# A hybrid encoder on one core: single-row norm, one addition ahead of a head, and wide products in two of the sample's projections

## The reference, cut to what matters

```
for layer in range(2):
    h = rms_norm(x, norm_mix)
    y = even mixer (S5 and GLA heads) @ ev_w_out    # layer 0
    y = diff_attention(h, od_w_in, ...) @ od_w_out  # layer 1
    x = x + y
    h = rms_norm(x, norm_cross); x = x + cross_attention(h, rms_norm(mem), x_w_q, x_w_kv, x_w_o)
    h = rms_norm(x, norm_mlp);   x = x + square(relu(h @ mlp_w1)) @ mlp_w2

def diff_attention(h, w_in, ...):
    q, k, v = split(h @ w_in, 3)                    # 1024 columns each
    q = rms_norm(q per head and half, 64 wide) * 64 ** -0.5
    k = rms_norm(k per head and half, 64 wide)
    ...
def cross_attention(h, m, ...):
    q = rms_norm(h @ w_q per head, 256 wide) * 256 ** -0.5
```

## Time and profile before

| | |
|---|---|
| median of 3 runs | 2398.26 us (2398.01 to 2398.31) |
| the profiled execution | 2397.84 us |
| its span, first to last instruction | 2396.1 us |
| TensorE matmuls busy | 2384.5 us (100%), 13751 of them |
| TensorE weight loads busy | 2019.0 us (84%) |
| VectorE busy | 1548.1 us (65%), 2626 instructions |
| ScalarE busy | 1169.3 us (49%), 2070 instructions |
| granted TensorE clock | 1.00 of full speed |

### The profile page before, as it was taken

The page is one execution under the profiler, slowest core; times in us unless marked ns, Lnnn a source line. Parts: engine busy times, 40 slices in busy tenths (PEclk is TensorE's granted clock), DMA queues, the critical chain, the costliest instruction groups (busy, mean ns, idle before and its releaser), DMA issues.

```text
span 2396.1 us, 34669 instructions
## 1 busy us (share of the span) xinstructions
PE 2384.5 (100%) x13751; PEld 2019.0 (84%) x13751; DVE 1548.1 (65%) x2626; ACT 1169.3 (49%) x2070; POOL 0.2 (0%) x4
## 2 busy tenths in 40 slices
PE   9999999999999999999999999999999999999999
PEld 6988877888889888998788888888888898888887
DVE  8999668776577876664665448858985565533332
ACT  5334455555435565545453436636764453533432
POOL 0000000000000000000000000000000000000000
PEclk9999999999999999999999999999999999999999
DMA  5445533563224553443234223233234323423322
GB/s 201 106 98 163 211 110 96 171 205 117 69 88 150 193 189 127 134 140 98 79 96 168 88 94 122 93 97 97 91 104 146 118 80 120 126 97 97 97 97 88
DMA packets 109696, 291.30 MB, mean 122 GB/s; under 512 B 18944, under 2 KB 40576, under 8 KB 108256
## 3 DMA queue, kind: packets, MB, share of 16 engines
q1 hardware_dynamic: 100832, 264.83, 34.6%
q10 hardware_dynamic: 8704, 24.25, 3.2%
HBM read 267.45 MB, written 19.50 MB: 120 GB/s over the span
## 4 chain that ended last, share of the span: by engine, by line
PE 86%; DVE 3%; ACT 1%; issue 0%; DVEq 0%; ACTq 0%
PE ps L1524 65%; PE ps L1510 5%; PE ps L1515 3%; PE ps L1638 2%; PE ps L1595 2%; PE ps L1620 2%; PE ps L1662 1%; PE ps L1651 1%; DVE wlo L1486 1%; PE ps L1608 0%; DVE ringP L1929 0%; PE ps L1669 0%; PE ps L2034 0%; PE ps L2101 0%; PE ps L1538 0%
## 5 line engine op out<-in xcount | busy, mean ns | idle before, releaser
L1481 ACT ACTIVATE whi<-wraw 128x1024 fp32r<-128x1024 f32 x430 | 451.9, 1052 | 173.8 <-PE ps L1524 127.2
L1524 PE MATMUL ps<-in_hP,whi 128*128 128x512 f32 x1336 | 533.2, 399 | 1.7 <-DVE in_lP L1936 0.9
L1486 DVE TENSOR_TENSOR wlo<-wraw,whi 128x1024 fp32r<-128x1024 f32 x430 | 522.3, 1217 | 0.2
L1524 PE MATMUL ps<-in_hP,wlo 128*128 128x512 f32 x1336 | 520.9, 390 | 0.0
L1524 PE MATMUL ps<-in_lP,whi 128*128 128x512 f32 x1336 | 520.2, 389 | 0.0
L1524 PE MATMUL ps<-hid_P,whi 128*128 128x512 f32 x1024 | 316.9, 391 | 0.0
L1524 PEld LDWEIGHTS ps<-in_hP,whi 128*128 128x128 f32 x1336 | 250.8, 188 | 60.5 <-issue 5.9
L1524 PEld LDWEIGHTS ps<-in_hP,wlo 128*128 128x128 f32 x1336 | 250.7, 188 | 53.4
L1524 PEld LDWEIGHTS ps<-in_lP,whi 128*128 128x128 f32 x1336 | 251.0, 188 | 51.8 <-issue 1.4
L1524 PE MATMUL ps<-in_S,whi 128*128 128x256 f32 x1536 | 285.4, 287 | 0.5 <-DVE x L1869 0.5
L1869 DVE TENSOR_TENSOR x<-ps,x 128x256 f32<-128x256 f32 (+1 forms) x192 | 106.7, 556 | 261.2 <-PE ps L1524 259.5
(11 more groups left out here) (506 smaller groups left out, 3509.1 us busy)
## 6 DMA issues: line engine op xcount, KB each, us to landing
wraw<-wt SPq DMA_DIRECT2D x432, 512.0 KB, 3.5
wraw<-wt ACTq DMA_DIRECT2D x17, 512.0 KB, 4.1
k_scratch<-region_P SPq DMA_DIRECT2D x16, 256.0 KB, 3.1
v_scratch<-vtmp SPq DMA_DIRECT2D x32, 128.0 KB, 3.6
x<-x_in SPq DMA_DIRECT2D x4, 768.0 KB, 6.7
x<-x_in SPq DMA_DIRECT2D x2, 1536.0 KB, 7.1
mix_mem<-mem_in ACTq DMA_DIRECT2D x1, 2048.0 KB, 15.2
region_S<-k_scratch ACTq DMA_DIRECT2D x2, 1024.0 KB, 7.5
```

The source lines that it names most:

```text
L1481: nc.scalar.activation(whi[:, (n + 3) % NHI, :, :], wraw[:, ws(n), :, :], ACT.Copy).then_inc(wh.sem, 1)
L1486: nc.vector.tensor_tensor(wlo[:, ws(n), :, :], wraw[:, ws(n), :, :], whi[:, (n + 3) % NHI, :, :].bitcast(F32), ALU.subtract).then_inc(wr.s ...
L1524: last = nc.tensor.matmul(ps[:, m % 2, 0:N[prod.g]], w_[:, k, :], x_[:, k, :], start=(k == 0 and j == 0), stop=(k == KT - 1 and j == 2))
```

## The change

It has four parts. (1) `WIDE` gains `q1` and `din`, and `Product` lets kinds "q" and "qkv" of the sample be wide. So the sample's queries of the second layer (8 tiles) and the 24 tiles of the differential input projection take the wide form. The halves are added by a VectorE reduce (`dve_halves`), which writes queries and keys to where ScalarE's copy went, and values to `ring`; it also frees the bank. ScalarE then squares from SBUF, and does not copy any more. The residue of the square moves from the tile's own place on VectorE to the slot behind it (`dve_square_low`). (2) The prompt's norm ahead of its `q1` is cut in `ONES` and no longer in `FINE`. (3) `added` holds also beside a "fin" of the prompt, which is the case for the first sample tile of `eo` alone. (4) In a slot where the step of a query pair goes first, a wide tile is taken first too; no wide tile stands in such a slot.

```diff
-            WIDE = {WT[n] for n in ("dn00", "dn01", "dn02", "dn03", "dout", "o0", "up01", "up02", "up03", )}
+            WIDE = {WT[n] for n in ("dn00", "dn01", "dn02", "dn03", "dout", "o0", "up01", "up02", "up03", "q1", "din", )}
...
-                    if g == "S" and kind in ("res", "up") and w0 in WIDE:
+                    if g == "S" and kind in ("res", "up", "q", "qkv") and w0 in WIDE:
...
             run(Product("res", "P", WT["dout"], dP.ready, norm=nP))
-            later([], *norm_steps(nP, FINE))
+            later([], *norm_steps(nP, ONES))
             mS.run(10)
...
+                elif prod.kind == "q" and prod.wide is not None:
+                    a.wait_ge(tf[b].sem, m // 2 + 1)
+                    if i >= 2:
+                        a.wait_ge(z["tqd"].sem, prod.tq + i // 2)
+                    nc.scalar.activation(ring[g][:, i % 2, :], qx[g][:, i, :], ACT.Square).then_inc(z["sqd"].sem, 1)
...
+                elif prod.kind == "qkv" and prod.wide is not None:
+                    if i < 16:
+                        a.wait_ge(tf[b].sem, m // 2 + 1)
+                        if i >= 2:
+                            a.wait_ge(z["ssum"].sem, prod.stats[i - 2].sum)
+                        act_chain(nc.scalar.activation(ring[g][:, i % 2, :], (dq, dk)[i // 8][g][:, i % 8, :], ACT.Square))
+                        if i >= 1:
+                            a.wait_ge(z["ssum"].sem, prod.stats[i - 1].sum)
+                        nc.scalar.activation(sq_h[g][:, :], ring[g][:, i % 2, :], ACT.Copy).then_inc(z["sqd"].sem, 1)
...
+            def dve_halves(v, t, to):
+                prod, i, m = t
+                b = m % 2
+                v.wait_ge(td.sem, m + 1)
+                nc.vector.tensor_reduce(to, ps[:, b, :].rearrange("p (z t) -> p t z", z=2), AX.X, ALU.add).then_inc(tf[b].sem, 1)
+
+            def dve_square_low(v, t):
+                prod, i, m = t
+                v.wait_ge(gs["S"]["sqd"].sem, prod.sq + i + 1)
+                nc.vector.tensor_tensor(sq_l["S"][:, i % 2, :], ring["S"][:, i % 2, :], sq_h["S"][:, :].bitcast(F32), ALU.subtract)\
+                    .then_inc(gs["S"]["sql"].sem, 1)
...
+                elif prod.kind == "q" and prod.wide is not None:
+                    dve_halves(v, t, qx[g][:, i, :])
+                elif prod.kind == "qkv" and prod.wide is not None and i < 16:
+                    dve_halves(v, t, (dq, dk)[i // 8][g][:, i % 8, :])
+                elif prod.kind == "qkv" and prod.wide is not None:
+                    if i < 18:
+                        v.wait_ge(z["ssum"].sem, prod.stats[i - 2].sum)
+                    else:
+                        v.wait_ge(z["vtr"].sem, prod.vtr + i - 17)
+                    dve_halves(v, t, ring[g][:, i % 2, :])
...
-                            step[0] == "nfin" and step[1].g == "P" for step in steps)
+                            step[0] == "nfin" and step[1].g == "P" or step[0] == "fin" and step[1].g == "P" for step in steps)
...
+                        if before is not None and before[0].kind == "qkv" and before[0].wide is not None and before[1] < 16:
+                            dve_square_low(v, before)
                         if added:
                             dve_tile(v, t)
                         done = q_first(t, steps)
+                        if done and t[0].wide is not None:
+                            dve_tile(v, t)
...
-                        if t is not None and not added:
+                        if t is not None and not added and not (done and t[0].wide is not None):
                             dve_tile(v, t)
```

## The result

| | before | after |
|---|---|---|
| median | 2398.27 us (2398.01 to 2398.89) | 2401.7 us (2401.52 to 2403.5) |
| ratio, 95% interval | | 1.0016 (1.0009 to 1.0023) |
| span of the profiled execution | 2396.1 us | 2399.8 us |

The account below looks back on a forecast made before the run. TensorE bounds the kernel by its issue, not by waits. Projection +5.2, second queries -0.7, norm -1.0 and head -0.3 make +3.2 us on 2398.26: 2401.5 us, range 2397.5 to 2405.0.

Parts of the forecast that it names:

- TensorE is the bound by the starts of its tiles: Whole kernel: TensorE is busy 2384.5 of 2396.1 us, so the distance between tile starts and idle time before them count.
- A wide tile gives 0.09 us: Projection and second sample queries: a wide tile takes 2.79 us on TensorE instead of 2.88.
- Rival (d): All 32 wide tiles: each takes 2.86 us instead of 2.79, total +5.4 us, 2403.7; chance 0.01.
- The chain over VectorE makes a three 12.35 us: Projection's query and key tiles: the order on VectorE makes each three last 12.35 us, not 11.52; before it was 11.70.
- Rival (a): Projection: the chain is hidden after all, VectorE's 9.8 us of work fits; total -4.2 us, 2394.1; chance 0.10.
- Rival (b): Projection: the chain is longer than its parts, 12.9 us per three, total +6.5 us, 2404.8; chance 0.20.
- The projection costs 5.2: Differential input projection: 5.9 us lost up to the last query or key sum, 0.7 given back by value tiles.
- The three small terms: Second sample queries wide -0.7 us, norm in single rows -1.0, x ahead of the last head -0.3.
- The norm gives 1.0: Norm before the prompt's q1: single rows keep VectorE's slots at 2.73 us and remove TensorE's 0.89 idle, gaining 1.0.
- The head gives 0.3: Last head: adding x before its five instructions starts the eighth tile at 503.83 instead of 504.17, gaining 0.3 us.
- Rival (c): Norm and head: the two small edits give nothing, VectorE being as late one tile on; +4.5 us, 2402.8; chance 0.10.
- both legs: Projection three: first sum to second, equal to TensorE's cover at 6.3 us; second to next first, about 0.8 wait.

Follow-up runs that it names:

- the mended three: One projection three (two sample tiles, one prompt tile) in the kernel called both moves, lasting 11.52 us where the changed kernel takes 12.40.
- The experiment that freed the second leg: Changed kernel with the first tile's VectorE reduce moved ahead of its slot's weight residue (wlo): 2401.77 us; also called the first reduce early.
- the second residue early: Changed kernel with the residue of the second tile's square moved ahead of the first tile's root and scaling: 2402.55 us.
- both moves: Changed kernel with the first tile's reduce ahead of its slot's weight residue and the second square's residue right behind its reduce: 2395.12 us.
- the root first: Changed kernel with the first tile's reduce ahead of its weight residue, and ScalarE's first root ahead of the second tile's square: 2394.96 us.

## Why the prediction was right, point by point

- **TensorE is the bound by the starts of its tiles.** Right. A window without a wait goes by its tiles alone: 11.48 us for a value three (forecast 11.5), 11.52 for the mended three.
- **A wide tile gives 0.09 us.** Right. The queries went from 24.35 to 23.75, 0.6 us for eight tiles, where 0.7 were set down; 0.18 for a three of value tiles (11.66 to 11.48). By the isolated issue gap of the Trainium skill (TensorE: Matmul & The Clock Gate, Back-to-back issue gap), as an estimate, the eight tiles would have gained 0.17 us; the same section says that a stream of weight loads and matmuls is spaced otherwise than this formula. The windows show 0.6. Rival (d) is out with it.
- **The chain over VectorE makes a three 12.35 us.** Right, at 12.40. The links are as forecast: residue to sum 0.56 (1001.82 to 1002.38), wlo 1.14 (998.95 to 1000.09), reduce to the next instruction 0.60. TensorE loses the 0.8 us ahead of each first sum that were forecast, of which the profile counts 0.65 as idle. The second sum does not wait, but with a thin reserve: its residue starts at 1007.51, so by the same 0.56 it could have started at 1008.07, and it starts at 1008.16 (6.34 behind the first residue, forecast 6.3). The forecast for the second three was 2.05 us lost; its first sum came at 977.58 against 975.65, where the stage had started 0.11 earlier: 2.04. Rival (a), that 9.8 us of work fit into 11.7, is out: VectorE is busy for 9.52 of 12.40, and order, not amount, makes the difference. Rival (b) would have needed 12.62.
- The Trainium skill (VectorE: DVE Perf Modes, The DRAIN you can't avoid) has the pipe empty ahead of each next instruction; taken alone, as the prediction took it, that made 12.9 us. The same section adds that a next instruction that is not held starts earlier, which the prediction left out. An earlier start is what the trace shows: the wlo of 1.22 us is followed after 1.14 (998.95 to 1000.09), and the three took 12.40.
- **The projection costs 5.2.** A little low: 5.45 by the kernel without it, 5.6 by the starts of the changed kernel's tiles, 5.7 to 5.9 by the kernel with it alone. From the first sum of the second three to that of the eighth, 6 times 0.70 in place of 0.65 are 0.3 more; the three was sized 0.05 us short. The three small terms are each off by about 0.1 or less.
- **The norm gives 1.0.** It gave 1.12 at the place; VectorE is full there (11.53 of 11.53 us in the last of the four windows under the result), and yet each slot comes out at 2.73, as forecast:

```profile
1868.60 1.23 DVE L1486 TENSOR_TENSOR wlo<-wraw,whi 128x1024 fp32r<-128x1024 f32 x1
...
1871.33 1.23 DVE L1486 TENSOR_TENSOR wlo<-wraw,whi 128x1024 fp32r<-128x1024 f32 x1
```

- **The head gives 0.3.** Right, for the reason given. x is added at 486.21 (forecast 485.95), and VectorE, without a pause behind it, keeps the delay, so that the sixth tile's x comes at 503.44 (forecast 503.28, in an execution whose tiles start 0.2 later from the outset). The third tile starts 0.65 us earlier, measured from the first, and at the ninth 0.3 of it is left. Rival (c) is out with both.

```profile
486.21 0.42 DVE L1895 TENSOR_TENSOR x<-ps,x 128x256 f32<-128x256 f32 x1 [1.82 <-PE ps L1524]
...
503.44 0.42 DVE L1895 TENSOR_TENSOR x<-ps,x 128x256 f32<-128x256 f32 x1
```

What the prediction did not draw from its own count: that both legs must be short at once. It went once around, found the leg from the first sum to the second as long as TensorE's cover and the other 0.8 us longer, which is enough for the time of this kernel. It was not enough to tell what would mend it. The experiment that freed the second leg took the first for safe. There the second reduce had come behind a wlo, and with it the first root, which in ScalarE's queue stands behind square and rounding of the second tile, as the prediction itself had counted it; the expectation missed by 7 us.

## What to carry to other kernels

When an edit puts more on an engine that has room, follow the order and not the busy share: look which result the bounding engine waits for, and whether it now stands behind an instruction that itself waits for the bounding engine. What such a ring over several engines costs is set by the longest way once around it: a move that frees one place may just push the wait to the next, and two moves that give nothing alone can give all together. Put work that must be early into the pause in which its engine waits for another, and count the order in every engine's queue that the ring passes through.

## What the runs showed of the hardware that was not expected

Behind a single pause of TensorE of about 2.1 us its granted clock fell to half in some executions and not in others. In the kernel with the second residue early, the pause was 2.12 us both in a profile without a fall (first) and in one with it (second, another execution):

```profile
977.75 0.36 PE L1559 MATMUL ps<-sq_hS,ones_r 128*128 128x256 f32 x1 [2.12 <-DVE sq_lS L1883]
```

```profile
977.74 0.36 PE L1559 MATMUL ps<-sq_hS,ones_r 128*128 128x256 f32 x1 [2.12 <-DVE sq_lS L1883]
```

By the share of the microsecond in which the clock fell (0.80 and 0.84), the fall came at about 978.6 (projection alone) and 978.7 us (second residue early); the pauses had ended at 978.14 and 977.74, so TensorE was at work again. Of the changed kernel's 17 executions 4 took about 2403.5 us at 0.999, of the kernel with the projection alone 4 of 8, of the one with the second residue early 5 of 11, all with this pause, 2.05 to 2.12 us in their profiles. With the pause down to 0.99 (both moves, or the root first) none of 22 executions was at 0.999. Nor was any of the 11 with the first reduce early, whose threes are as long (12.45) and which has a wait of 0.68 in each from the third on. Its longest wait for a residue in this stage is this one:

```profile
982.87 0.35 PE L1559 MATMUL ps<-sq_hS,ones_r 128*128 128x256 f32 x1 [0.90 <-DVE sq_lS L1883]
```

Apart from the first matmul of the program, TensorE waits nowhere else for another engine for more than 0.9 us in the traces of the kernel before, the changed one and the two with a fall. So it is the single long pause that goes with the fall, and not the slow threes. The two profiles with a fall and these counts speak for the pause as its cause; what decides from one execution to the next stays open. The kernel before, with a pause of 0.21 in this place, also had two of its 101 executions at 0.999 (2400.83 and 2400.78 us), of which there is no profile.
